# Three loads at the head of a hybrid attention and mLSTM block move to other issue queues

## The reference, cut to what matters

```python
h = rms_norm(x, pre_norm_g[l])                 # x * rsqrt(mean(x^2) + eps) * g
proj = jnp.einsum('bsd,dc->bsc', h, w_in[l])
aq, ak, av, az, mq, mk, mv, mo, mz, mi, mf = split_columns(proj)
ya = moba_attention(rope(aq), rope(ak), av);  ya = rms_norm(ya, g_a) * silu(az)
ym = sigmoid(mo) * norm(mlstm_chunkwise(silu(conv(mq, mk)), mv, mi, mf)) * silu(mz)
y = jnp.einsum('bsc,cd->bsd', concat([ya, ym]), w_out[l])
x = x + rms_norm(y, post_norm_g[l])
```

## Time and profile before

| | us |
|---|---|
| median of 3 runs | 314.51 (314.25 to 314.8) |
| profiled execution | 314.27 |
| its span | 312.5 |
| TensorE matmul busy | 306.0 (98% of the span) |
| VectorE, ScalarE, GpSimd busy | 226.8, 165.2, 91.1 |

### The profile page before, as it was taken

The page is one execution under the profiler, slowest core; times in us unless marked ns, Lnnn a source line. Parts: engine busy times, 40 slices in busy tenths (PEclk is TensorE's granted clock), DMA queues, the critical chain, the costliest instruction groups (busy, mean ns, idle before and its releaser), DMA issues.

```text
span 312.5 us, 5011 instructions
## 1 busy us (share of the span) xinstructions
PE 306.0 (98%) x1607; PEld 257.4 (82%) x1607; DVE 226.8 (73%) x510; ACT 165.2 (53%) x339; POOL 91.1 (29%) x110
## 2 busy tenths in 40 slices
PE   8999999999999999999999999999999999999992
PEld 5788888888888888888888899977888888888892
DVE  2644899956999499967999457996666867856534
ACT  3467694578337324384244583574746867353301
POOL 4501005164340004000040017569612983000000
PEclk9999999999999999999999999999999999999997
DMA  7933473565423546752555432410210473310111
GB/s 208 338 77 96 105 203 100 159 196 143 151 67 97 157 144 183 215 168 72 156 184 155 130 103 67 135 69 1 81 55 2 139 222 125 141 51 0 69 68 67
DMA packets 28953, 38.28 MB, mean 123 GB/s; under 512 B 2552, under 2 KB 16236, under 8 KB 28928
## 3 DMA queue, kind: packets, MB, share of 16 engines
q1 hardware_dynamic: 27440, 34.51, 37.2%
q0 software_dynamic: 1328, 3.32, 3.0%
q10 hardware_dynamic: 160, 0.14, 0.1%
HBM read 33.68 MB, written 4.28 MB: 121 GB/s over the span
## 4 chain that ended last, share of the span: by engine, by line
PE 94%; issue 3%; DVE 0%; DVEq 0%; ACT 0%; POOLq 0%; POOL 0%; ACTq 0%
PE bank L1516 25%; PE bank L1518 24%; PE bank L1517 24%; PE bank L1569 4%; PE bank L1873 3%; PE bank L1817 3%; PE bank L1838 3%; PE bank L1664 2%; PE bank L1767 1%; PE bank L1531 1%; PE bank L1549 1%; PE bank L1828 1%; PE bank L1665 1%; PE bank L1850 0%; PE bank L1542 0%
## 5 line engine op out<-in xcount | busy, mean ns | idle before, releaser
L797 ACT ACTIVATE w_hi<-w_raw 128x512 fp32r<-128x512 f32 (+1 forms) x73 | 44.4, 615 | 62.9 <-PE bank L1518 50.1
L1516 PE MATMUL bank<-w_hi,xT_hi 128*128 128x512 f32 (+2 forms) x180 | 71.1, 395 | 0.0
L1518 PE MATMUL bank<-w_hi,xT_lo 128*128 128x512 f32 (+2 forms) x180 | 68.1, 379 | 0.0
L1517 PE MATMUL bank<-w_lo,xT_hi 128*128 128x512 f32 (+2 forms) x180 | 67.8, 376 | 0.0
L1516 PE MATMUL bank<-xT_hi,w_hi 128*128 128x512 f32 x136 | 54.1, 397 | 0.0
L1072 DVE TENSOR_TENSOR w_lo<-w_raw,w_hi 128x512 fp32r<-128x512 f32 (+1 forms) x66 | 46.5, 715 | 9.7 <-ACT w_hi L797 9.5
L1518 PE MATMUL bank<-xT_hi,w_lo 128*128 128x512 f32 x136 | 53.3, 392 | 0.0
L1517 PE MATMUL bank<-xT_lo,w_hi 128*128 128x512 f32 x136 | 53.1, 391 | 0.0
L1518 PEld LDWEIGHTS bank<-w_hi,xT_lo 128*128 128x128 f32 x180 | 33.8, 188 | 5.8
L1516 PEld LDWEIGHTS bank<-w_hi,xT_hi 128*128 128x128 f32 x180 | 34.0, 189 | 5.0 <-POOL w_lo L685 0.4
L1517 PEld LDWEIGHTS bank<-w_lo,xT_hi 128*128 128x128 f32 x180 | 34.0, 189 | 4.5
(11 more groups left out here) (213 smaller groups left out, 568.8 us busy)
## 6 DMA issues: line engine op xcount, KB each, us to landing
w_raw<-in_w_in SPq DMA_DIRECT2D x66, 256.0 KB, 2.9
w_raw<-in_w_out SPq DMA_DIRECT2D x16, 256.0 KB, 2.6
farena<-g_rows POOLq DMA_DIRECT2D x4, 640.0 KB, 4.2
kq_rows<-stage SPq DMA_DIRECT2D x8, 256.0 KB
gy<-kq_rows SPq DMA_DIRECT2D x8, 256.0 KB, 3.3
gy<-in_x SPq DMA_DIRECT2D x4, 512.0 KB, 5.0
out_y<-gy SPq DMA_DIRECT2D x7, 256.0 KB, 2.1
w_raw<-in_w_in SPq DMA_DIRECT2D x8, 196.0 KB, 3.3
```

The source lines that it names most:

```text
L797: a.activation(hi, raw, ACT.Copy).then_inc(w_hi_done, 1)
L1516: pe.matmul(o, hi, m_hi, start=start, stop=False)
L1517: pe.matmul(o, hi, m_lo, start=False, stop=False)
L1518: return pe.matmul(o, lo, m_hi, start=False, stop=stop)
```

## The change

The load of weight block 0 leaves SyncE's loop and is issued by ScalarE's queue in place of the pre-norm weights; these are issued by GpSimd's queue ahead of the identity matrix. What is loaded, where to, and what waits for it stays as it is.

```diff
@@ SyncE
             for n, (mat, kind, k, c) in enumerate(SLOTS):
                 if n in X_BEFORE:
                     load_x(X_BEFORE[n])
+                if n == 0:
+                    continue
                 if n >= RAW:
                     low_done(sp, n - RAW)
@@ GpSimd
+            g.dma_start(prow[:], rows_of(pre_g)).then_inc(par_in, 16)
             g.memset(ident[:], 0.0).then_inc(cleared, 1)
             g.memset(prow2[:], 0.0).then_inc(par2_clear, 1)
             g.wait_ge(cleared, 1)
@@ ScalarE
-            a.dma_start(prow[:], pre_g.rearrange("o (c p) -> (o c) p", p=P)).then_inc(par_in, 16)
+            first_cols = SLOTS[0][3]
+            a.dma_start(w_raw[:, 0, :], w_in[0, 0:P, first_cols:first_cols + AW]).then_inc(raw_in[0], 16)
             a.activation(ssx[:, 0:1], ones, ACT.Copy)
             x_hi_half(0)
             x_hi_half(1)
```

## The result

| | before | changed |
|---|---|---|
| median | 314.8 us | 317.97 us (317.88 to 318.63) |
| ratio, 95% interval | | 1.0102 (1.0074 to 1.013) |
| profiled execution | 314.27 | 317.88 |
| its span | 312.5 | 316.1 |
| TensorE matmul busy | 306.0 | 306.8 |

The median before is that of five executions here, 314.51 was that of three. Two loads change their queue, weight block 0 and the pre-norm weights; x chunk 0, the third of the title, keeps its own.

A forecast was written before the change was run, and what follows sets the result against it. TensorE was taken to bound the kernel, with no later slack for a late start. x late +0.7, pre-norm weights +0.1, faster clock -0.1 made +0.7 on 314.27: 315.0, or 315.2 as a median; 8-in-10 range 314.3 to 317.2.

The forecast's parts named there:

- Where the head is bound, and that nothing behind can swallow a late start: First microseconds: TensorE alone is the chain, 94% of the whole chain, so a late start counts in full.
- Block 0 earlier is worth 0.0: Slot 0's start: TensorE's own queue binds until 5.09 and xT_hi until 4.93, so an earlier block saves 0.0 us.
- x chunk 0 late by 0.7, at most by 0.8: Head loads: two queues share the DMA engines, x lands up to 4.5 instead of 3.7; +0.7 us taken.
- The pre-norm weights land at 3.3 to 4.3, adding 0.1: GpSimd's load at the head: against x chunk 0 at 4.4 it adds 0.0 to 0.15 us, 0.1 taken.
- the quiet row: Profile row of GpSimd's small transfer at DMA share 0.41: 1.8 us, lower bound giving a landing at 2.6.
- the row of 5.4 us: Profile row of GpSimd's first small loads at DMA share 1.11: 5.4 us, upper bound giving a landing at 6.2.
- A late start gives back 0.1 by the clock: Slot 0's first four matmuls: started at 5.9 they find the faster rate, 1.02 us instead of 1.15; -0.1.
- the pre-norm weights come late: Rival at the head: landing 5.4 us after issue, at 6.2, delays x's transposes; +2.5 us, 317.0, chance 0.20.
- the clock rises later: Rival in slot 0: TensorE's 0.7 us pause keeps it at 1.2 GHz longer; +0.7 + 1.5, 316.7, chance 0.15.
- The sum for TensorE's filling matmuls: TensorE's head: filling matmuls end at 3.75 + 0.91 + 0.43 = 5.09, with transposes at half of 0.43 each.
- The Trainium skill's rule on issuing engines: DMAs of all issuing engines interleave on the same 16 engines; wins at most 0.5 us, summing to +0.7.
- SyncE's queue, the identity matrix, ScalarE's issue: Head side effects: later SyncE loads gain 0.0, identity has 1.2 us of cover, ScalarE's issue loses nothing.

The follow-up runs named there:

- e6: The changed kernel without the load of the pre-norm weights (prow set to 1.0 by a GpSimd memset): 316.56 us, ratio 1.0044 to the kernel before.
- e2: The kernel before with only weight block 0 moved to ScalarE's queue, ahead of the pre-norm weights, which stay on that queue: 316.9 us, ratio 1.0064.
- e5: The changed kernel with 15 filling matmuls in place of 6 at TensorE's head: 316.79 us against the changed kernel's 317.97.
- e4: The kernel before with the pre-norm weights on GpSimd's queue and all SyncE loads held until they have landed: one execution, 317.57 us.
- e3: The kernel before with weight block 0 moved to ScalarE's queue, issued behind the pre-norm weights, which stay there: 315.28 us, ratio 1.0013.
- e7: The changed kernel with TensorE transposing x chunk 0 ahead of the pre-norm weights: 318.81 us, ratio 1.0111 to the kernel before.

## Why the prediction was wrong, step by step

- *Where the head is bound, and that nothing behind can swallow a late start*: right. +3.61 at slot 1 and +3.6 in the span.
- *Block 0 earlier is worth 0.0*: right. It landed at 0.82 + 3.7 = 4.5, no sooner than before, although issued 0.5 us earlier.
- *x chunk 0 late by 0.7, at most by 0.8*: mis-sized. It measured +1.5 (4.4 us to landing in the changed kernel against 2.9, and +1.6 at its transposes in e6). The step that failed is "at most when both had ended before": I took the rate of one queue, 280 GB/s, for the first microsecond of two, and an even share. Measured were 111 GB/s in the changed kernel and 143 to 160 in e2, e5 and e6, where x got as many bytes as block 0. So it is the rate that failed; x came late with an even share as well as without.
- *The pre-norm weights land at 3.3 to 4.3, adding 0.1*: this is the step that failed most. They landed at 6.3. The sum started from the quiet row's 1.8 (right for idle engines: 1.9 in e4) and added too little for the load (1.7 for 512 KB, which is 1.9 at the rates named); the row of 5.4 us, which I kept as an upper bound, was the nearer one (5.0). The issue also began 0.5 later than GpSimd was free.
- *A late start gives back 0.1 by the clock*: wrong in sign. It cost 0.8 us in the profile. In the changed kernel the later start did not find the rate already up; with filling matmuls through the pause (e5) it did. e3 is the one case that went as I had reasoned: a start 1.1 later, and slot 0 0.1 shorter.
- *The rivals*: "the pre-norm weights come late" (+2.5, 317.0) and "the clock rises later" (+1.5 on top of what delays it) were each what happened, and I priced them as alternatives. They are cause and effect: a load that is late enough to matter makes TensorE pause. The first rival's +2.7 at x's transposes and the 0.8 measured for the clock give 3.5 of the 3.6. The clock rival's own +1.5 is twice what this execution lost, and within the 0.8 to 1.9 of the table. The range was too narrow for the same reason.
- *The sum for TensorE's filling matmuls*: 5.09 is right, but the 0.91 in it is the timeline's, from 3.75 to the filling matmuls at 4.66; the half of 0.43 named there would give 0.86 for four.
- *The Trainium skill's rule on issuing engines* ("DMA: Bandwidth & Descriptors", section "Issuing engines are not separate DMA queues") held in its direction: two queues brought nothing. That the loads interleave fits e2, e5 and e6, and hardly the 62 against 14 packets of the changed kernel. *The fixed 2.0 us* of the Trainium skill, same page, section "Anatomy of one DMA — SWDGE (gpsimd) path" agrees with e4's 1.9 and the quiet row's 1.8; under load 3.2 and 5.0 were measured.
- *SyncE's queue, the identity matrix, ScalarE's issue*: hidden, as predicted; the identity was done by 2.9 and first used at 6.4.

## What to carry to other kernels

A small load on which the first wait depends should be issued before the large ones, on a queue where nothing large stands ahead of it: first on ScalarE's queue it was there by 3.5 (before, e3). Its time to landing grew with what the DMA engines held: 1.9, 3.2 and 5.0 us for the same 4 KB from GpSimd's queue, 4.0 behind 256 KB on ScalarE's. Where a kernel waits in its first microseconds, price the wait with the clock: waits of 0.9 to 2.9 us cost another 0.8 to 1.9 in eight of nine kernels, and filling matmuls through the wait gave that back in e5. When two rivals are cause and effect, put their sum in the range.

## What was not expected of the hardware

- Two loads issued at the same moment from SyncE and ScalarE moved fewer bytes together than one did alone: 111 to 160 GB/s from 2 to 3 us in five kernels, against 276. How they shared differed between executions of the same loads: 62 against 14 packets between 2 and 3.1 us in the changed kernel, equal bytes in e5. Why the rate falls stays open; no run separated block 0's wider packets (2 KB against 512 bytes) from its queue. Packets of that width aren't slow at every time: block 0 moved 0.11 MB in 75.5% of the engines' time from 2 to 3 us in the changed kernel, and as much in 39.0% from 3 to 4 us in e3.
- GpSimd's first DMA as its first instruction begins at 1.33, where a memset in its place begins at 0.80.
- TensorE can lose the fast rate again within some 2 us: fast at 5.35 and slow at 7.44 in e7. In e2 it was fast at 5.56, after the wait, and the second four matmuls of slot 0 were slow, with no wait between them and the first four.
